# Norm sums from three bfloat16 terms in a Hymba-style decoder layer on eight cores: the split put between other work, and the final norm two groups later

## The reference, cut to what matters

```python
def rmsnorm(x, g):
    xf = x.astype(jnp.float32)
    xf = xf * lax.rsqrt(jnp.mean(xf * xf, axis=-1, keepdims=True) + EPS)
    return xf.astype(x.dtype) * g
...
        h = rmsnorm(x, g_mix[i])
        proj = h @ w_in[i]                                   # (B, S, D_IN)
...
        x = x + y @ w_out[i]
...
        h2 = rmsnorm(x, g_ffn[i])
        a = jax.nn.relu(h2 @ w_ff1[i])
        x = x + (a * a) @ w_ff2[i]
    return rmsnorm(x, g_final)
```

## Time and profile before

| | |
|---|---|
| times of three executions | 1574.13, 1574.82, 1576.72 us (median 1574.82) |
| the profiled execution's own time | 1575.38 us |
| its span on the slowest core (core 6) | 1574.3 us; the cores lie between 1563.0 and 1574.3 us |
| TensorE matmul busy | 1526.9 us, 97% of the span |
| VectorE, ScalarE, GpSimd busy | 941.3 us (60%), 737.9 us (47%), 145.1 us (9%) |
| mean granted TensorE clock of the eight cores | 0.992 to 0.996 |

### The profile page before, as it was taken

The page is one execution under the profiler, slowest core; times in us unless marked ns, Lnnn a source line. Parts: engine busy times, 40 slices in busy tenths (PEclk is TensorE's granted clock), DMA queues, the critical chain, the costliest instruction groups (busy, mean ns, idle before and its releaser), DMA issues.

```text
span 1574.3 us, 28153 instructions; the slowest of 8 cores (1563.0 to 1574.3 us)
## 1 busy us (share of the span) xinstructions
PE 1526.9 (97%) x9732; PEld 758.9 (48%) x9732; DVE 941.3 (60%) x1426; ACT 737.9 (47%) x1128; POOL 145.1 (9%) x198
## 2 busy tenths in 40 slices
PE   5989999999999999999999999999999999999997
PEld 2434545544455445554455444554455444554446
DVE  5557567645566647556466546657476555656665
ACT  5646654533645335543536336443545335444225
POOL 2001111101111011011001010001100000100001
PEclk8999999999999999999999999999999999999999
DMA  9877576787879486686657583355634363433642
GB/s 273 201 227 245 149 155 126 131 211 235 194 164 194 142 304 154 135 245 204 206 145 233 162 284 134 108 188 169 245 134 161 135 229 133 158 137 141 207 169 73
DMA packets 46986, 285.03 MB, mean 181 GB/s; under 512 B 5760, under 2 KB 11008, under 8 KB 15488
## 3 DMA queue, kind: packets, MB, share of 16 engines
q1 hardware_dynamic: 30336, 179.32, 33.0%
q0 software_dynamic: 15504, 103.62, 28.4%
q10 hardware_dynamic: 1008, 0.30, 0.1%
HBM read 283.55 MB, written 46.92 MB: 210 GB/s over the span
## 4 chain that ended last, share of the span: by engine, by line
PE 91%; DVE 3%; DMA 2%; ACT 2%; issue 2%; DVEq 0%; POOL 0%; ACTq 0%; SPq 0%; POOLq 0%
PE mm L393 77%; PE ob L732 7%; PE sc L707 4%; PE sc L393 2%; DMA ring<-wall 1%; DMA X<-xh 1%; DVE acc L424 1%; ACT sq L414 0%; PE mm L1050 0%; ACT Vd L398 0%; DVE X L924 0%; DVE h2T L457 0%; DVE X L457 0%; ACT acc L433 0%; ACT P L414 0%
## 5 line engine op out<-in xcount | busy, mean ns | idle before, releaser
L393 PE MATMUL mm<-h2T,ring 128*128 128x512 bf16 (+1 forms) x2192 | 502.1, 378 | 1.8 <-ACT KT L398 0.7
L393 PE MATMUL mm<-aT,ring 128*128 128x512 bf16 (+2 forms) x2208 | 461.5, 361 | 5.6 <-DVE aT L874 2.2
L709 ACT ACTIVATE P<-sc 128x1024 bf16<-128x1024 f32 x256 | 247.6, 1021 | 184.5 <-PE sc L707 183.5
L393 PEld LDWEIGHTS mm<-h2T,ring 128*128 128x128 bf16 x2192 | 204.1, 98 | 240.2 <-issue 16.4
L393 PEld LDWEIGHTS mm<-aT,ring 128*128 128x128 bf16 x2208 | 201.1, 98 | 208.4 <-issue 8.6
L714 DVE TENSOR_TENSOR P<-P,E 128x1024 bf16<-128x1024 bf16 x224 | 154.4, 692 | 190.3 <-ACT P L709 190.2
L867 ACT ACTIVATE rt<-mm 128x512 f32<-128x512 f32 x232 | 138.3, 596 | 219.6 <-PE mm L393 173.0
L874 DVE TENSOR_TENSOR aT<-rt 128x512 bf16<-128x512 f32 x232 | 167.2, 734 | 75.8 <-ACT rt L867 74.0
L414 ACT ACTIVATE sq<-X 128x512 f32<-128x512 f32 (+2 forms) x196 | 118.4, 610 | 159.1 <-DVE X L903 90.1
L393 PE MATMUL mm<-hT,ring 128*128 128x512 bf16 x672 | 149.4, 384 | 5.0 <-ACT Vd L398 5.0
L424 DVE TENSOR_TENSOR acc<-acc,sq 128x512 f32<-128x512 f32 (+1 forms) x142 | 101.0, 711 | 60.9 <-ACT sq L414 59.7
(11 more groups left out here) (125 smaller groups left out, 964.8 us busy)
## 6 DMA issues: line engine op xcount, KB each, us to landing
ring<-wscratch SPq DMA_DIRECT2D x125, 1024.0 KB, 6.1
ring<-wall POOLq DMA_DIRECT2D x43, 1024.0 KB, 10.4
wscratch<-ring SPq DMA_DIRECT2D x21, 1024.0 KB, 7.1
X<-xr POOLq DMA_DIRECT2D x16, 1024.0 KB, 10.6
out<-X POOLq DMA_DIRECT2D x14, 1024.0 KB, 11.1
X<-xh POOLq DMA_DIRECT2D x12, 1024.0 KB, 13.1
X<-xh SPq DMA_DIRECT2D x6, 1024.0 KB, 19.0
vscratch<-Vd POOLq DMA_DIRECT2D x24, 192.0 KB, 8.2
```

The lines of the kernel that those rows point to most:

```text
L393: T.op("pe", lambda: nc.tensor.matmul(out_ap, lhsT=l, rhs=r, start=(i == 0), stop=(i == n - 1)), reads=rd, writes=[b_out], mark=(i == n - 1))
L709: T.op("act", lambda: nc.scalar.activation(out=P_[:], in_=s_[:], func=AF.Exp, scale=0.125), reads=[bs_], writes=[bP_])
```

## The change

A `stat` of the middle tiles no longer multiplies `acc` in float32. Ahead of it `acc` is split into three bfloat16 terms: `high(0)` copies `acc` to bf16 on ScalarE, `rest(0)` subtracts that copy from `acc` on VectorE, `high(1)` copies the rest to bf16, and `rest(1)` writes what is then left as the third term. The sum is three bf16 matmuls with a bf16 matrix `ones_b`. The four steps are side items of their own; where they stand, and by how much the sums and norms that follow are moved, is shown by the numbers in the diff. Changed are six `f_` and six `ln2` (stage I of tiles 5 to 10) and six `a2` (stage K of tiles 4 to 9), 18 sums in all; the halo tiles, tile 4's own `ln2` and tile 11 keep the float32 sum.

```diff
+        ones_b = sb("ones_b", [128, 128], BF16)
...
+            def splits(self, two):
+
+                (ta, bta), (tb, btb) = [(t_[:, 0:TOK].bitcast(BF16), b_) for t_, b_ in two]
+                t = [(ta[:, 0:TOK], bta), (ta[:, TOK:2 * TOK], bta), (tb[:, 0:TOK], btb)]
+
+                def high(i):
+                    T.op("act", lambda: nc.scalar.copy(out=t[i][0], in_=self.acc), reads=self.b_acc, writes=[t[i][1]])
+
+                def rest(i):
+                    out, b_ = (self.acc, self.b_acc) if i == 0 else (t[2][0], [btb])
+                    T.op("dve", lambda: nc.vector.tensor_tensor(out=out, in0=self.acc, in1=t[i][0], op=ALU.subtract),
+                         reads=[t[i][1]] + self.b_acc, writes=b_)
+                    if i == 1:
+                        self.terms = t
+                return [lambda: high(0), lambda: rest(0), lambda: high(1), lambda: rest(1)]
...
-                mm_ops(m_[:, 0:self.n], bm_, [(ones[:], self.acc, [b_ones] + self.b_acc)])
+                if self.terms is None:
+                    mm_ops(m_[:, 0:self.n], bm_, [(ones[:], self.acc, [b_ones] + self.b_acc)])
+                else:
+                    mm_ops(m_[:, 0:self.n], bm_, [(ones_b[:], t_, [b_ones, b_]) for t_, b_ in self.terms])
...
-                side += [(11, ln2.stat)] + [(12 + 0.5 * k, lambda k=k: ln2.norm(k)) for k in range(8)]
-                if f_ is not None:
-                    side += [(3, f_.stat)] + [(3.5 + k, lambda k=k, f_=f_: f_.norm(k)) for k in range(8)]
-                    side += [(7.6, lambda j=j: store(j - 1, 0)), (11.6, lambda j=j: store(j - 1, 1))]
+                if f_ is None:
+                    side += [(11, ln2.stat)] + [(12 + 0.5 * k, lambda k=k: ln2.norm(k)) for k in range(8)]
+                else:
+                    side += list(zip((9.2, 9.7, 10.1, 10.6), ln2.splits(SQ)))
+                    side += [(12, ln2.stat)] + [(13 + 0.5 * k, lambda k=k: ln2.norm(k)) for k in range(8)]
+                    side += list(zip((1.5, 2.2, 2.6, 3.6), f_.splits([(rt[i], b_rt[i]) for i in range(2)])))
+                    side += [(5, f_.stat)] + [(5.5 + k, lambda k=k, f_=f_: f_.norm(k)) for k in range(8)]
+                    side += [(9.6, lambda j=j: store(j - 1, 0)), (13.6, lambda j=j: store(j - 1, 1))]
...
                     side += ln_side(a2, 6.2, 2, 33.5, 35.2, 1.2)
+                    side += list(zip((24, 25, 26, 28), a2.splits(SQ)))
```

More of the change, by code:

```diff
@@ L235, in build_nc @@
         T.op("dve", lambda: nc.vector.memset(ones[:], 1.0 / D), writes=[b_ones])
+        T.op("dve", lambda: nc.vector.memset(ones_b[:], 1.0 / D), writes=[b_ones])
         T.op("act", lambda: nc.scalar.activation(out=sq[0][:, 0:1], in_=ones[:, 0:1], func=AF.Square),
@@ L407, in __init__ @@
                 self.sq = SQ_EARLY if early else SQ
-                self.first = None
+                self.first = self.terms = None
             def square(self, k):
```

## The result

The changed kernel takes 1584.85 us (median of 5 executions, 1581.6 to 1585.75) against 1574.82 us before (1574.13 to 1576.72): ratio 1.0057, 95% interval 1.0046 to 1.0068, 10.0 us slower. The forecast was 1584.5. The profiled execution took 1585.0 us, its slowest core is core 4 with a span of 1583.9 us.

The account below looks back on a forecast made before the run. TensorE's stream was taken to bound the kernel: 10.7 us lost at `f_`, 0.8 back at `a2`, 0 at `ln2`, rounded to 9.7 us slower, gave 1584.5 us; range 1580.5 to 1590.5, the forecast's own 1582 to 1587.

Parts of the forecast that it names:

- TensorE bounds the middle tiles: Middle tiles: TensorE streams with one 1.3 us wait from 384 to 1440 us, so any added wait costs its length.
- The chain at `f_`: Stage I: `rest(0)`, `high(1)`, `ln2`'s square, its addition and two adds delay g5; 1.78 us a tile, 10.7 us in all.
- The row for the hand-over: Profile row behind the assumed 0.17 us from ScalarE's end to VectorE's start, used in timing the `f_` split.
- Neither bound: Limits on the `f_` loss from cheaper or dearer `rest` steps: 1.2 to 2.1 us a tile, 7 to 13 us for six.
- `ln2` gives nothing: Stage I: K's first group waits for the V evacuation's bank, so the slot stays 1.04 us; 0 given back.
- `a2` gives 0.13 us: Stage K: the group after attention can start at 829.00 instead of 829.13; 0.13 us a tile, 0.8 us over six.
- A float32 sum takes 0.96 us: The slot behind `a2` was read as the matmul's own length; three bf16 matmuls at 0.65 us would save 0.31 us.
- The sum: Total over six tiles: 10.7 - 0.8 + 0 = 9.9 us, rounded down to 9.7 us slower for what `ln2` may give.
- The gain of the matmuls: Rival, all 18 sums: the matmuls' gain shows and the split hides; 5.6 us back, 1569.2 us; chance 0.06.
- Half the chain: Rival at `f_`: split instructions far cheaper than float32 ones, 0.3 us a tile left, no change within 3 us; chance 0.05.
- The clock: Rival at the new `f_` waits: TensorE's granted clock falls, 1.7 us each, one to six falls give 1586 to 1595; chance 0.15.
- a named sign of being wrong: Stated signs: g5 follows g4 within 1.2 us, ScalarE's CAST starts before g2's add ends, or the clock rows fall.

Follow-up runs that it names:

- the square's swap: The changed kernel with the second `ln2` square ahead of `high(1)` on ScalarE, same instructions: 1574.06 us, ratio 0.9992 against the kernel before.
- the own bank: The kernel before with its float32 `f_` and `ln2` sums in a free score bank of attention's: 1572.69 us, ratio 0.9981.
- the edits that take the chain and the banks away: The changed kernel with the square ahead of `high(1)`, `f_` and `ln2` sums in a score bank, `ln2` sum one group later: 1567.92 us, ratio 0.9955.

## Why the prediction was right, point by point

- **TensorE bounds the middle tiles; what it waits comes out as time.** Right: the 1.42 us a tile are, within 0.01 us, those of the slots.
- **The chain at `f_`.** Right in every link and in its order, and shown by the square's swap. Its size was 1.78 us and measured 1.64: the hand-over from ScalarE is 0.10 us rather than 0.17, and the rest of the difference lies in steps of VectorE and ScalarE that are 0.01 to 0.02 us shorter each. The row for the hand-over, 713.13 to 713.30, was one case among others. Neither bound was reached: a bf16 operand made the subtraction neither shorter nor longer than the add (0.69 us).
- **`ln2` gives nothing.** Right: 1.04 us, set by the V evacuation, and 0.65 us once it had a bank of its own and, one group later, time for `rest(1)`.
- **`a2` gives 0.13 us.** Mis-sized: 0.21 us a tile. My earliest start of the next group, 829.00, took ScalarE's evacuation as fixed; with the change it starts 0.54 instead of 0.66 us after the sum's start and ends in time, so that the group starts 0.55 us after attention, as before. Why ScalarE is earlier is not shown.

```profile
833.96 0.58 ACT L888 ACTIVATE rt<-mm 128x512 f32<-128x512 f32 x1
```

- **A float32 sum takes 0.96 us.** Mis-sized: 0.86 us. The 0.96 us from the sum to attention held 0.10 us that belong to the change to attention's matmuls; three bf16 matmuls in the same place take 0.74 instead of 0.65. So the most that the terms could give back was 0.21 us a sum, 3.8 us in all, and not 5.6. Here the Trainium skill was the better source: FP8 and Floating Point Precision, section TensorE Precision Notes, gives true float32 four passes, and the estimate from it, 4 x 0.216 = 0.86 us, is what the own bank shows.
- **The sum.** Six times 1.64 - 0.21 is 8.6 us against 9.7 forecast, as the chain was put 0.14 us too long and `a2` 0.08 us too low in each tile. The measured 10.0 us holds 1.3 us or so from outside these tiles, which the sum does not have, so part of the closeness is luck.
- **Rivals.** The gain of the matmuls (chance 0.06) did not show; it does with the edits that take the chain and the banks away: 1.05 us a tile, 0.63 of it the matmuls' (three times 0.21) and the rest the banks'. Half the chain (0.05) is out, since both subtractions take 0.69 us. The clock (0.15) stayed at 1.00 on core 4, which set the time; a fall there was a named sign of being wrong. It did fall elsewhere: of the 48 such pairs of waits (six tiles, eight cores) two, on cores 2 and 5, both in tile 6, were followed by a stretch that is partly at the lower level (1.2 GHz); of the 48 pairs of the run with only `f_` changed none was. Core 5 (from:to us, length, TensorE busy, matmuls, PEclk, DMA share, GB/s):

```profile
537.00:540.50 3.50, 1.92 (x8) 1.00 0.84 295
540.50:545.00 4.50, 4.41 (x13) 0.62 0.01 5
545.00:549.00 4.00, 4.00 (x21) 1.00 0.13 18
```

4.5 x 0.38 = 1.7 us there, as the rival priced it (tile 6 takes 183.4 us on these two cores and 181.7 us on the others), but on cores that were not the slowest.

## What to carry to other kernels

Before making a short matmul between two groups shorter, look whether the group behind it starts on the matmul's end or on a bank: with two banks in turn the slot is the evacuation of the group ahead (1.04 to 1.10 us here), and another bank (0.43 us a tile here) is worth nearly as much as a faster matmul (0.63). A step that hands a value from VectorE to ScalarE and back should have nothing behind it in either queue that a third engine waits for; one place in the order was worth 1.5 us a tile. When an item in a full queue is moved, check what it comes to stand between, as the last norm between K's evacuations.

## What the runs showed of the hardware that was not expected

A 128x128x512 float32 matmul in the stream takes 0.86 us against 0.216 us in bf16, four times. A VectorE subtraction with a bf16 operand and one with a bf16 output take the same 0.68 to 0.69 us as the all-float32 add, and ScalarE's copy of float32 to bf16 takes 0.62 us, its square 0.63 us. With eight cores at work a bf16 matmul of 512 columns started every 0.216 us, at a granted clock of 1.00, through the middle tiles of the slowest core, before and after the change.
